# Stick-breaking query rows of the samples: spread by a 0/1 product and a ScalarE copy in place of a DRAM store and broadcast loads

## The reference, cut to what matters

```python
def _stick_breaking(q, k, v, q_pos):
    z = jnp.einsum('bqhd,bshd->bhqs', q, k).astype(jnp.float32) * HEAD_DIM ** -0.5
    strict = (jnp.arange(L, dtype=jnp.int32)[None, :] < q_pos[:, None])[None, None]
    log_keep = jnp.where(strict, jax.nn.log_sigmoid(-z), 0.0)
    after = lax.cumsum(log_keep, axis=3, reverse=True) - log_keep
    a = jnp.where(strict, jnp.exp(jax.nn.log_sigmoid(z) + after), 0.0)
    o = jnp.einsum('bhqs,bshd->bqhd', a.astype(v.dtype), v)
```

## Time and profile before

| | us |
|---|---|
| runs of the kernel before | 735.66, 736.65, 739.93 |
| their median | 736.65 |
| span of the profiled execution | 733.5 |
| TensorE busy | 608.8 |
| VectorE busy | 377.3 |
| ScalarE busy | 149.7 |

### The profile page before, as it was taken

The page is one execution under the profiler, slowest core; times in us unless marked ns, Lnnn a source line. Parts: engine busy times, 40 slices in busy tenths (PEclk is TensorE's granted clock), DMA queues, the critical chain, the costliest instruction groups (busy, mean ns, idle before and its releaser), DMA issues.

```text
span 733.5 us, 8305 instructions
## 1 busy us (share of the span) xinstructions
PE 608.8 (83%) x3304; PEld 343.3 (47%) x3304; DVE 377.3 (51%) x667; ACT 149.7 (20%) x284; POOL 111.7 (15%) x100
## 2 busy tenths in 40 slices
PE   3997899899889968997679997388996977979673
PEld 2874684478678844543558545222322312223221
DVE  3049999898959998732003133742341422414024
ACT  2113104421420254445100010021101101010101
POOL 1613613211111342642200000000000000000001
PEclk9998989999999987999859998589999999899997
DMA  9998879948976388999979595119999999999941
GB/s 330 408 408 336 315 261 356 394 174 312 363 257 240 127 329 297 331 427 428 422 245 404 196 358 193 38 60 360 404 392 396 401 389 405 385 404 395 399 192 60
DMA packets 116929, 230.91 MB, mean 315 GB/s; under 512 B 14235, under 2 KB 82347, under 8 KB 106620
## 3 DMA queue, kind: packets, MB, share of 16 engines
q1 hardware_dynamic: 100556, 138.23, 51.6%
q0 software_dynamic: 12672, 88.09, 30.3%
q10 hardware_dynamic: 3664, 4.10, 1.8%
HBM read 225.77 MB, written 4.61 MB: 314 GB/s over the span
## 4 chain that ended last, share of the span: by engine, by line
PE 36%; SPq 23%; DVE 17%; DMA 14%; ACT 4%; issue 3%; ACTq 1%; POOL 1%; DVEq 0%
SPq L443 20%; PE PS L591 10%; DVE arena L1571 5%; DMA arena<-in_cache_v_a,page_idx 4%; PE PS L1009 4%; DVE x_rows L1575 4%; DMA arena<-in_w_down 4%; PE PS L1025 4%; SPq L447 3%; DMA arena<-in_cache_v_b,unit_idx 2%; PE PS L1085 2%; PE PS L935 2%; PE PS L712 2%; DMA temp<-in_cache_k_a,page_idx 2%; PE PS L1149 1%
## 5 line engine op out<-in xcount | busy, mean ns | idle before, releaser
L591 PE MATMUL PS<-xT,arena 128*128 128x264 f32 x608 | 144.3, 398 | 5.1 <-ACT arena L1335 4.7
L591 PEld LDWEIGHTS PS<-xT,arena 128*128 128x128 f32 x608 | 117.4, 195 | 27.1 <-ACT arena L1335 5.3
L1571 DVE TENSOR_TENSOR arena<-arena,x_rows 128x2048 f32<-128x2048 f32 x32 | 73.1, 2283 | 28.9 <-DMA x_rows<-q_dram 28.8
L1575 DVE TENSOR_REDUCE x_rows<-arena 128x32 f32<-128x2048 f32 x32 | 73.2, 2288 | 1.1
L520 POOL DMA_INDIRECT arena<-in_cache_k_b,unit_idx x32 | 39.7, 1239 | 147.1 <-DVE x_rows L1575 142.3
L1149 PE MATMUL PS<-arena,temp 128*32 128x512 f32 x256 | 38.5, 756 | 23.2 <-DMA arena<-in_w_down 20.5
L2018 DVE TENSOR_TENSOR x_rows<-PS,x_rows 128x512 f32<-128x512 f32 (+1 forms) x48 | 33.0, 687 | 43.1 <-PE PS L1109 43.1
L1109 PE MATMUL PS<-temp 128*128 128x512 f32 (+1 forms) x96 | 47.2, 628 | 4.5 <-issue 4.5
L1101 PE MATMUL PS<-arena,temp 128*32 128x512 f32 x384 | 45.8, 610 | 4.4 <-issue 3.3
L520 POOL DMA_INDIRECT arena<-in_cache_v_b,unit_idx x32 | 39.2, 1226 | 54.2 <-PE PS L935 33.5
L581 POOL TENSOR_TENSOR small<-small,consts 128x1 f32<-128x1 f32 x3 | 2.6, 867 | 274.6 <-DVE small L2070 274.6
(11 more groups left out here) (342 smaller groups left out, 856.2 us busy)
## 6 DMA issues: line engine op xcount, KB each, us to landing
arena<-in_w_down SPq DMA_DIRECT2D x32, 1024.0 KB, 10.5
arena<-in_w_gate SPq DMA_DIRECT2D x48, 512.0 KB, 7.7
arena<-in_w_up SPq DMA_DIRECT2D x48, 512.0 KB, 7.9
arena<-in_w_in SPq DMA_DIRECT2D x9, 2048.0 KB, 11.7
temp<-in_w_gate SPq DMA_DIRECT2D x12, 512.0 KB, 9.9
temp<-in_w_up SPq DMA_DIRECT2D x12, 512.0 KB, 8.1
temp<-in_w_out SPq DMA_DIRECT2D x1, 4096.0 KB, 15.3
x_rows<-in_x_prompt SPq DMA_DIRECT2D x2, 1024.0 KB
```

What stands on the lines that cost most here:

```text
L591: last = nc.tensor.matmul(PS[0:m, n % 2, 0:T], w[:, k, c0:c0 + m], xT[:, k, :], start=(k == 0), stop=(k == KC - 1))
L1571: nc.vector.tensor_tensor(k_ring[:, u], k_ring[:, u], q_all[:, b % 2:b % 2 + 1, :].to_broadcast([P, 4, H * HD]), ALU.mult).then_inc(s_mul, 1)
L1575: nc.vector.tensor_reduce(z_s[:, b, :].rearrange("p (h r) -> p r h", r=R)[:, 4 * u:4 * u + 4, :], k_ring[:, u].rearrange("p r (h d) -> p r ...
```

## The change

The store, the eight broadcast loads and `q_dram` go. A matrix `pick_row` (8 rows x 8 x 128 columns; block b has ones in row b and zeros elsewhere) is made once by VectorE from the identity. TensorE multiplies block b by the 8 query rows, which puts row b on all 128 partitions of a PSUM bank, and ScalarE copies the bank into `q_all`. The eight spreads take numbers of their own (`M_QB`) in the row of banks 2 and 3; `m_ka` renumbers the A keys around the fifth.

```diff
-        q_row = temp[0:NS, 8192:8704]
-        q_dram = nc.dram_tensor("q_dram", [NS, H * HD], F32).ap()
+        q_row = oaT.rearrange("p k t -> p (k t)")[0:NS, 0:H * HD]
+        pick_row = obT.rearrange("p k t -> p (k t)")[0:NS, 0:NS * P]
 SyncE
-            sp.wait_ge(s_qdram, 16)
-            for b in range(2):
-                sp.dma_start(q_all[:, b, :], q_dram[b:b + 1, :].to_broadcast([P, H * HD])).then_inc(s_q[b], 16)
             sp.wait_ge(s_proj, N_QI)
 TensorE
+            def spread_q(b):
+                m = M_QB[b]
+                pe.wait_ge(s_trf, max(m - 1, M_Q + 1))
+                nc.tensor.matmul(PS[:, 2 + m % 2, :], pick_row[:, b * P:(b + 1) * P], q_row, start=True, stop=True
+                                 ).then_inc(s_tr, 1)
+            pe.wait_ge(s_pick, 1)
+            spread_q(0)                       # behind L627
             ...
+            spread_q(1)                       # behind the index-query chunks
+            spread_q(2)                       # behind the last scoring of index keys
+            spread_q(3)                       # behind chunk QA + 3, ahead of count 1
+                    if x == 12:
+                        spread_q(4)           # in pair 1 of turn_ka
+            spread_q(5)                       # ahead of the wait for s_lgc
+            spread_q(6)                       # behind the rows, ahead of count 13
+                if c == 4:
+                    spread_q(7)               # gates, ahead of chunk 5 and of L805, L807
 ScalarE
-            act.dma_start(q_dram, q_row).then_inc(s_qdram, 16)
-            def load_q(b):
-                act.wait_ge(s_mul, 4 * (b - 1))
-                act.dma_start(q_all[:, b % 2, :], q_dram[b:b + 1, :].to_broadcast([P, H * HD])).then_inc(s_q[b % 2], 16)
+            def spread_q(b):
+                m = M_QB[b]
+                act.wait_ge(s_tr, m + 1)
+                if b >= 2:
+                    act.wait_ge(s_mul, 4 * (b - 1))
+                nc.scalar.copy(q_all[:, b % 2, :], PS[:, 2 + m % 2, :]).then_inc(s_trf, 1)
 VectorE
+            nc.vector.tensor_copy(pick_row.rearrange("p (b n) -> p b n", b=NS),
+                                  ident[0:NS, 0:NS].unsqueeze(2).to_broadcast([NS, NS, P])).then_inc(s_pick, 1)
             link(nc.vector.memset(pads[:, 0:608], 0.0))
 ...
-                    dve.wait_ge(s_q[b % 2], 16 * (b // 2 + 1))
+                    dve.wait_ge(s_trf, M_QB[b] + 1)
```

More of the change, by code:

```diff
@@ L335, in decoder_step @@
         s_v = [sem(f"s_v{u}") for u in range(8)]
-        s_q = [sem(f"s_q{i}") for i in range(2)]
-        s_qdram, s_mul, s_kused, s_ls, s_sps, s_scan, s_ts, s_as, s_vused, s_owide, s_apad0, s_apad1 = (
-            sem(n) for n in ("s_qdram", "s_mul", "s_kused", "s_ls", "s_sps", "s_scan", "s_ts", "s_as", "s_vused",
+        s_pick, s_mul, s_kused, s_ls, s_sps, s_scan, s_ts, s_as, s_vused, s_owide, s_apad0, s_apad1 = (
+            sem(n) for n in ("s_pick", "s_mul", "s_kused", "s_ls", "s_sps", "s_scan", "s_ts", "s_as", "s_vused",
                              "s_owide", "s_apad0", "s_apad1"))
@@ L367, in decoder_step @@
         vb_rows = a["cache_v_b"][0].rearrange("n (q r) h d -> (n q) (r h d)", r=4)
[L370 to L374, removed]
+        M_Q, M_QB = 0, [1, 2]
+        M_WI = 3
+        M_KIDX = 4
+        M_QB += [M_KIDX + 2 * NS, M_KIDX + 2 * NS + 1]
+        M_KA = M_QB[3] + 1
+        M_QB += [M_KA + 12, M_KA + 4 * NS + 1]
+        m_ka = lambda x: M_KA + x + (x >= 12)
+        M_ROWS = M_QB[5] + 1
+        M_QB += [M_ROWS + 12, M_ROWS + 13]
+        M_NEW = M_QB[7] + 1
         M_AFT = [M_NEW + 1, 0]
@@ L432, in _ @@
                     sp.wait_ge(s_bdram, 16)
-                    sp.wait_ge(s_tr, M_KA + 4 * NS)
+                    sp.wait_ge(s_tr, m_ka(4 * NS - 1) + 1)
                     for par in range(2):
@@ L548, in _ @@
                 if k == 15:
-                    pool.wait_ge(s_tr, M_KA + 8)
+                    pool.wait_ge(s_tr, m_ka(7) + 1)
                     fetch_ka(2)
                 if k == 17:
-                    pool.wait_ge(s_tr, M_KA + 16)
+                    pool.wait_ge(s_tr, m_ka(15) + 1)
                     fetch_ka(3)
@@ L707, in turn_ka @@
                 for which in range(2):
-                    m = M_KA + 8 * pair + 2 * j + which
+                    x = 8 * pair + 2 * j + which
+                    if x == 12:
+                        spread_q(4)
+                    m = m_ka(x)
                     pe.wait_ge(s_trf, m - 1)
@@ L721, in _ @@
                         turn_ka(pair, j + 1)
-                    m = M_KA + 8 * pair + 2 * j
-                    pe.wait_ge(s_trf, m + 2)
+                    pe.wait_ge(s_trf, m_ka(8 * pair + 2 * j + 1) + 1)
                     for which in range(2):
                         last = nc.tensor.matmul(PS[which * 32:(which + 1) * 32, ACC + j, :], qaPad[:, pair + 4 * which, :],
-                                                kT_s[:, 4 + m % 4 + which, :], start=False, stop=(pair == 3))
+                                                kT_s[:, 4 + 2 * j % 4 + which, :], start=False, stop=(pair == 3))
                     last.then_inc(s_kT2_used, 1)
@@ L1240, in _ @@
             relu_kidx(3)
-            load_q(2)
+            spread_q(2)
             for c in range(4):
                 evac(N_QA + c, qaT[:, c, :])
-            load_q(3)
+            spread_q(3)
             evac(N_KA, kaT)
@@ L1250, in _ @@
                 if j == 12:
-                    load_q(4)
-                m = M_KA + j
+                    spread_q(4)
+                m = m_ka(j)
                 act.wait_ge(s_tr, m + 1)
@@ L1255, in _ @@
                     act.wait_ge(s_kT2_used, j // 2 - 1)
-                nc.scalar.copy(kT_s[:, 4 + m % 4, :], PS[:, 2 + m % 2, :]).then_inc(s_trf, 1)
+                nc.scalar.copy(kT_s[:, 4 + j % 4, :], PS[:, 2 + m % 2, :]).then_inc(s_trf, 1)
             for j in range(4):
@@ L1261, in _ @@
             act.wait_ge(s_sc, 1)
-            load_q(5)
+            spread_q(5)
             for c in range(8):
@@ L1275, in _ @@
             act.wait_ge(s_trf, m)
-            load_q(6)
+            spread_q(6)
             for names, dst in zip(outs, places):
@@ L1336, in _ @@
                 if c == 4:
-                    load_q(7)
+                    spread_q(7)
                 if c == 7:
```

4 lines of the change are left out of this document (2 added, 2 removed).

## The result

Beside the kernel before, the changed kernel came out a little faster. Its median is 733.32 us (725.39 to 737.74, 20 runs); the kernel before, run beside it, has 737.51 us (729.93 to 741.28, 20 runs). The ratio is **0.9946, 95% interval 0.992 to 0.9971**: 4.0 us, from 2.1 to 5.9. The forecast was 730.5 us, or 6.1 us of gain, with a range of 726 to 737. So sign and range hold in this comparison, and the gain is two thirds of the forecast.

A forecast was written before the change was run, and what follows sets the result against it. TensorE was taken to set the time up to L807. Its gains less the spreads' costs left 6.1 us there, so the span went from 733.5 to 727.4, and with 3.15 around it the time to 730.5 us; range 726 to 737.

The forecast's parts named there:

- What bounds the kernel: Up to L807 at 217 us TensorE sets the time; the end moves by what TensorE has gained there.
- The price of a spread: Each spread costs TensorE 0.9 us, plus 0.59 us for ScalarE's copy of a bank.
- Step 1: VectorE's start: the pick copy takes 1.1 us (1.1 to 1.9) and delays everything by 0.6 us (0.6 to 1.5).
- Step 2: Unit 0 on VectorE starts at 36.9 instead of 47.06 us, a head start of 10.2 us.
- Steps 3 and 4: TensorE up to 84, then VectorE's first ask: 3.8 us gained at 76.5, count 0 at about 87.2, 5.1 ahead.
- signs of being wrong: Unit 4 not starting before 64, VectorE not waiting at L807, or the stretch behind 217 not as long as before.
- Step 5: Count 0 to pair 3 on TensorE: upper clock in 32 products gains 3.0 us; 8.3 us ahead at 150.
- Pair 3: TensorE's 2.15 us wait at 142.19 for this pair's loads: 1.4 us goes, plus 0.6 of low clock behind it.
- Step 6: From 150 us to L807: spreads 5, 6 and 7 cost 0.15, 1.15 and 0.9 us, leaving 6.1 us ahead.
- The clock rival: The clock gains don't come: without 3.0 us behind count 0 and 2.0 of pair 3, 735.5 us; chance 0.22.
- The slower rival: Late key units 4 to 8 eat the head start; TensorE keeps its wait and low clock: 740.6 us; chance 0.10.
- Behind 217: Nothing is changed after 217 us; that stretch moves along at the same length, costed at nothing.

The follow-up runs named there:

- the second set: Four programs beside the kernel before, on a chip of their own; the changed kernel again gave 1.0019, the kernel before again 0.997.

## Why the prediction was right, and where its size was off

**What bounds the kernel: right up to L807.** TensorE takes every product there whole: the kernel with ten products more showed it directly. And TensorE is what VectorE meets: with unit 4 earlier VectorE only waited elsewhere, and in all three traces of the change it still waits for L825 (L807 before), 2.4 us. That the end moves by what TensorE has won there was borne out by the ten added products, whose 15.0 us at the row were 14.3 us in the time, and not by the kernel with two samples by product, whose 4 us at the row didn't show in the time.

**The price of a spread: a little low.** 0.9 us was taken, from a row of products of 512 columns; 1.05 us is what a spread takes on TensorE where it stands alone, and 0.86 us what a further product adds. ScalarE's copy, taken at 0.59, is

```profile
39.60 0.58 ACT L1232 COPY x_rows<-PS 128x512 f32<-128x512 f32 x1 [1.27 <-PE PS L635]
```

**Step 1: too high.** The pick copy took 0.68 us, not 1.1, and moved VectorE's start by 0.34, not 0.6; on TensorE 0.2 us of it were left. The Trainium skill, VectorE: DVE Perf Modes, in "Mode 2×_2P", lets such a copy take two numbers a tick. The trace agrees with it: 1024 numbers took 0.68 us, less than even the faster of the two rows of before (264 numbers in 0.29) gives, and the range's other end, 1.9 us, is out.

**Step 2: right.** From the turning to unit 0 it was 47.06 - 33.34 = 13.7 us, and is 40.22 - 37.11 = 3.1. The path is 10.6 us shorter in this pair and 10.1 by the means of three (13.2 and 3.1); it was forecast at 10.2 + 0.6 = 10.8. The Trainium skill, DMA: Bandwidth & Descriptors, in its part on the two cost components, would have the old path at 2.0 us plus bytes over 436 GB/s per transfer, a fit that it gives for transfers issued by GpSimd; these were issued by ScalarE and SyncE. No trace here agrees with it: with the queues full the store took 4.48 and the load 7.96 us, and the path became 10 us shorter.

**Steps 3 and 4: right in mechanism, a little high.** One of the signs of being wrong came up: unit 4 was to start before 64 and started at 65.49. It did so because that execution turned the query rows at 37.11; in the third, undisturbed one it started at 61.78, where 61.7 was forecast. Counted from the turning, count 0 was to come 5.1 + 0.6 = 5.7 us earlier. It came 5.4 us earlier in the first pair of traces and 4.6 us by the means. The wait ahead of the small weights went in all three, and VectorE's new wait for L676 stood where it was expected. The 4.67 us ahead of the small weights belonged in part to the one trace of before: in the other two they were 1.55 and 3.76.

**Step 5 failed in size.** This is the term that makes most of the difference. It gave 3.2 us from count 0 to the end of the pairs (5.1 to 8.3), or 3.05 with spread 5. The first chunk behind them starts 116.8 us behind the turning before (119.8, 116.6, 114.0) and 111.3 now (112.1, 111.3, 110.4): 5.5 us earlier, of which 4.6 were won by count 0. So the step gave **0.9 us** where 3.05 were forecast. Its terms:

- The upper clock in the 32 products behind count 0: taken as 3.0. Those took 10.34, 9.72 and 7.37 us in the three traces of before and 7.37 in all of the change, so the mean is 1.8. The profiled execution of before had the worst of three.
- Spreads 3 and 4: 2.5, not 1.8. By the starts around them and those of the same rows before, spread 3 took 1.15 us and spread 4, with what it did to the products beside it, 1.36.
- Pair 3: waits of 2.15, 2.35 (in two pieces) and 0.19 us before, 0.46 and none now, so 1.4, as taken. Of the 0.6 for the clock behind it nothing is left on the mean: the first trace of before lost 1.3 us there and the others nothing, and the first trace of the change lost 1.2 us ahead of it, at 110.

These make 1.8 - 2.5 + 1.4 = 0.7 us, against 0.9.

**Step 6: right in sign, too dear.** From there to the row 32 x 8 the change lost 5.5 - 4.4 = 1.1 us instead of 2.05. The first output store goes out ahead of most of the copy and not behind it:

```profile
186.51 0.58 ACT L1232 COPY x_rows<-PS 128x512 f32<-128x512 f32 x1 [1.16 <-issue]
186.53 0.40 ACTq L1302 DMA_DIRECT2D out_k_a_p<-rows_kva  x1
```

One of the two waits for ScalarE around 200 is gone in the changed kernel (2.28 us are left in the first trace, 2.46 and 2.27 before).

**The sum.** From the turning to the row 32 x 8: forecast 6.7, measured 186.8 - 182.4 = 4.4 us. Less 0.2 for the copy it is 4.2, and the comparison gave 4.0. That they agree so well is luck, since the three comparisons scatter by more than the difference. The clock rival (735.5) was half right: of the 5.0 us that it took away, the 3.0 of step 5 were 1.8 and the 2.0 of pair 3 were 1.4. The slower rival didn't occur: unit 4 wasn't late by its keys. The "3.15 around the span" compare the median with another execution's span; every run has 1.75 to 2.0 us between its own span and its time. The forecast of the median doesn't hang on that: 736.65 - 6.1 is 730.5 either way.

**Behind 217: open.** It was costed at nothing. It took 509.2 us before and 511.7 now by the means, with 6.6 us between the extremes of one program, so neither nothing nor a loss of 2 us is excluded, and the latter would be half of what is won ahead of it. In the traces the start and this stretch vary most. The set at 1.0019 is that in which ScalarE stands still in every trace; why the changed kernel lost its gain there isn't shown. With two samples by product but no further gain in time, and 1.0113 for a mere change of order, the tail's share of the differences stays open too.

## What to carry over

Spreading a row over partitions by a 0/1 product makes a path shorter where a broadcast through DRAM is *waited for* (some 10 us here, with full queues, of which 4.6 reached TensorE at the next join), and costs about 1 us of TensorE per bank where it isn't; do it for the first rows and test the rest. A wait that is taken away comes back at the next join unless its cause moves: find who would be late next, and make that one earlier. And take no term of a sum from the clock of one trace: another execution of the same program gave 7.37 us for 10.34.

## What the runs showed of the hardware

- The record of the granted clock can read 1.00 while products run at half pace. In the first trace of the change, stretches of 2 us at the start of the 64 products (length, busy PE, PEld, DVE, ACT, POOL; clock, DMA share, GB/s), 5 or 6 products each, and then 11:

```profile
21.00:23.00 2.00, 2.00 (x6) 1.59 (x5) 0.00 (x0) 0.00 (x0) 1.70 (x2) 1.00 1.02 417
23.00:25.00 2.00, 2.00 (x6) 1.49 (x6) 0.00 (x0) 0.00 (x0) 1.39 (x3) 1.00 1.00 412
...
27.00:29.00 2.00, 2.00 (x11) 1.71 (x10) 0.00 (x0) 0.00 (x0) 1.60 (x2) 1.00 1.05 409
```

  This came in six of fourteen traces, of both programs' kinds, and cost 1.4 to 3.1 us.
- ScalarE can stand still for 3.6 to 7.4 us near the start for a reason the profile doesn't name (9.96 and 10.60 us of idle, above), in either program: in all four traces of the second set and in none of the other ten.
- The clock falls in full stretches, too. In five traces, all of kernels with products for samples 2 to 7, 32 products in a row that begin between 181 and 201 us took 8.70 to 10.27 us and not 7.37, and TensorE's longest wait since 160 had been 0.34 us; in three more such traces they took 7.37. From count 0 to the row 32 x 8 the kernel before had 0 to 10.5 us at the lower level, the changed one 2.6 to 7.7, and the one with ten products more 20.1. So added work can cost more than its length; that the change itself lost anything in this way isn't shown.
